# Block 2 of a three-block transformer kernel: gate panels first in the weight stream, head panels rounded at a head's opening, norm statistics in columns

## The reference, cut to what matters

```
u = layer_norm(h) * (1 + sc1) + sh1;   z = u @ w_in          # zq zf zi zg zu zv zga zgb
y_a = hgrn2_mixer(zq, zf, zi, zg) @ w_proj_a                 # 8 heads, a recurrence over 8 chunks
y_b = (gelu(zu) * (W_s LN(gelu(zv)) + b)) @ w_proj_b         # gMLP mixer
mix = (sigmoid(zga + b_a) * y_a + sigmoid(zgb + b_b) * y_b) @ w_out
h   = layer_norm(ALPHA * h + g1 * mix) * ln1_w + ln1_b
```

## Time and profile before

| | us |
|---|---|
| runs | 3443.26, 3445.19, 3452.99 (median 3445.19) |
| profiled execution, its own time | 3450.49 |
| span of its instructions | 3448.7 |
| PE busy | 3134.7 (91%) |
| DVE, ACT, POOL busy | 1843.9 (53%), 1605.0 (47%), 735.3 (21%) |
| granted PE clock, mean | 0.946 of full |
| block 2 up to `out2` | about 813 to 1505 of the span |

### The profile page before, as it was taken

The page is one execution under the profiler, slowest core; times in us unless marked ns, Lnnn a source line. Parts: engine busy times, 40 slices in busy tenths (PEclk is TensorE's granted clock), DMA queues, the critical chain, the costliest instruction groups (busy, mean ns, idle before and its releaser), DMA issues. The chain is left out here.

```text
span 3448.7 us, 38856 instructions
## 1 busy us (share of the span) xinstructions
PE 3134.7 (91%) x13848; PEld 2405.1 (70%) x13848; DVE 1843.9 (53%) x2196; ACT 1605.0 (47%) x2147; POOL 735.3 (21%) x381
## 2 busy tenths in 40 slices
PE   7987899998989888779999884999999999999997
PEld 6754678786777666658888664777777777777753
DVE  3256433426354303361031545888878878888864
ACT  4334444423565322232232422766667666666652
POOL 3400234442323242324444330000000000000020
PEclk9987999999999889899999995999999999999998
DMA  3243322222211021212222614999999999999971
GB/s 142 98 171 117 117 84 97 98 88 84 74 72 50 25 110 49 98 49 97 95 93 106 271 49 197 356 405 400 404 407 402 404 404 398 409 400 403 406 275 49
DMA packets 65734, 694.19 MB, mean 201 GB/s; under 512 B 6928, under 2 KB 7312, under 8 KB 25584
## 3 DMA queue, kind: packets, MB, share of 16 engines
q1 hardware_dynamic: 54480, 650.57, 48.0%
q0 software_dynamic: 7056, 25.69, 1.9%
q10 hardware_dynamic: 4112, 16.78, 1.2%
HBM read 654.74 MB, written 38.27 MB: 201 GB/s over the span
## 5 line engine op out<-in xcount | busy, mean ns | idle before, releaser
L141 POOL TENSOR_TENSOR ring_low<-ring,mix_ring_high 128x1024 fp32r<-128x1024 f32 x120 | 295.3, 2493 | 518.2 <-ACT mix_ring_high L136 518.2
L202 PE MATMUL psum<-mix_high,mix_ring_high 128*128 128x512 f32 x864 | 350.1, 405 | 31.9 <-PEq L1815 11.2
L204 PE MATMUL psum<-mix_high,ring_low 128*128 128x512 f32 x864 | 341.6, 395 | 0.0
L202 PE MATMUL psum<-ex_high,ex_rows_high 128*128 128x512 f32 x768 | 318.3, 414 | 6.8 <-DVE ring_low L2647 6.8
L204 PE MATMUL psum<-ex_high,ex_rows_low 128*128 128x512 f32 x768 | 305.8, 398 | 0.0
L203 PE MATMUL psum<-h_low,mix_ring_high 128*128 128x512 f32 x736 | 291.6, 396 | 0.0
L136 ACT ACTIVATE mix_ring_high<-ring 128x1024 fp32r<-128x1024 f32 x124 | 121.0, 1048 | 334.0 <-DMA ring<-wstream 334.0
L141 POOL TENSOR_TENSOR ring_low<-ring,ff_ring_high 128x1024 fp32r<-128x1024 f32 x72 | 174.8, 2463 | 419.6 <-ACT ff_ring_high L136 227.5
L2478 POOL CAST ex_index<-table 128x1 uint32 x32 | 6.0, 187 | 1083.1 <-PE psum L2496 1083.1
L2647 DVE TENSOR_TENSOR ring_low<-ring,ex_high 128x2048 fp32r<-128x2048 f32 x96 | 214.3, 2287 | 40.3 <-ACT ex_high L2589 40.3
L2647 DVE TENSOR_TENSOR ex_more_low<-ex_more,ex_high_in_x 128x2048 fp32r<-128x2048 f32 x96 | 219.6, 2287 | 22.0 <-ACT ex_high_in_x L2589 22.0
(11 more groups left out here) (551 smaller groups left out, 6897.5 us busy)
## 6 DMA issues: line engine op xcount, KB each, us to landing
ex_more<-moe_w SPq DMA_DIRECT2D x128, 2048.0 KB, 9.4
ring<-wstream SPq DMA_DIRECT2D x87, 2048.0 KB, 8.0
ring<-moe_w SPq DMA_DIRECT2D x64, 2048.0 KB, 10.6
ex_bias_up<-moe_b SPq DMA_DIRECT2D x32, 1024.0 KB, 11.1
y_rows<-ex_y SPq DMA_DIRECT2D x33, 512.0 KB, 10.9
y_rows<-mx_zero ACTq DMA_DIRECT2D x1, 16384.0 KB, 50.0
x<-xt SPq DMA_DIRECT2D x8, 256.0 KB, 4.8
rel<-rel_bias SPq DMA_DIRECT2D x1, 2048.0 KB, 10.4
```

The costliest lines, as they stand in the source:

```text
L141: e.tensor_tensor(low, full, high.bitcast(F32), ALU.subtract).then_inc(self.low_ready, 1)
L202: pe.matmul(out, a[0], b[0], start=start, stop=False)
L204: return pe.matmul(out, a[1], b[0], start=False, stop=stop)
```

## The change

The gate panels come first in each pair of the stream (gate, projection, gate, projection). The first gate panel of mixa is multiplied in body 7 of `hgrn_stage`, as its `following` products; that of mixb in `gmlp_stage` behind L1854, bank by bank as `biased` allows. The gates go to banks 0 to 3 and the projections to 4 to 7; `mix_stage` keeps the panels 1, 2, 3. One more panel load is issued in each of the two stages in front. ACT rounds ring panel n+2 of the head loop at the opening of body n, between taking tile 0 and tile 1 of head n+1, and no longer ahead of the squares. In `gmlp_stage` the gated result `zu` is split tile by tile (ACT highs, DVE lows). The ACT order in `mix_stage` has the four sigmoids ahead of the rounding of panels 2 and 3. `Norm` is new: PE turns the sums into columns (four matmuls of one column for each row of sums, the tokens on partitions), the statistics are made on 128x4, and each is spread again by DVE making four 128x128 diagonals and PE four matmuls of 128 columns with ones. Only n6 keeps the old form (`WideNorm`). In `zi`, the raw norm is spread behind the first four products, and PE's tile 5 waits for `raw_scaled`.

```diff
@@ class Norm (new; the old one is kept as WideNorm)
+    def add_stats(self, pe, tile, at):
+
+        for t in range(TT):
+            mm = pe.matmul(self.stat[:, at + t:at + t + 1], tile[:, t * P:(t + 1) * P], self.g.ones_mean[:, 0:1],
+                           start=True, stop=True)
+        return mm
+
+    def spread(self, pe):
+        if self.centre:
+            for t in range(TT):
+                pe.wait_ge(self.mean_diag, t + 1)
+                mm = pe.matmul(self.mean[:, t * P:(t + 1) * P], self.g.ones, self.diag(0, t), start=True, stop=True)
+            mm.then_inc(self.averaged, 1)
+        for t in range(TT):
+            pe.wait_ge(self.rstd_diag, t + 1)
+            mm = pe.matmul(self.rstd[:, t * P:(t + 1) * P], self.g.ones, self.diag(1, t), start=True, stop=True)
+        mm.then_inc(self.rstd_ready, 1)
+
+    def averages(self, pe):
+        for row in self.rows:
+            mm = self.add_stats(pe, self.g.sums[:, row, :], row * TT)
+        mm.then_inc(self.stat_ready, 1)
+        self.spread(pe)
+
+    def raw_spread(self, pe):
+        for t in range(TT):
+            pe.wait_ge(self.raw_diag, t + 1)
+            mm = pe.matmul(self.raw[:, t * P:(t + 1) * P], self.g.ones, self.diag(0, t), start=True, stop=True)
+        mm.then_inc(self.raw_ready, 1)
+
+    def root(self, act):
+        g = self.g
+        act.wait_ge(self.var_ready, 1)
+        act.activation(self.std, self.var if self.centre else self.square_col, ACT.Sqrt,
+                       bias=g.eps[self.eps if self.before is None else "both"]).then_inc(self.std_ready, 1)
+        if self.before is not None:
+            act.activation(self.raw_std_col, self.raw_col, ACT.Sqrt, bias=g.eps[EPS_RMS]).then_inc(self.raw_std, 1)
+
...
+    def spread_diag(self, dve, i, column, sem):
+        for t in range(TT):
+            dve.tensor_scalar(self.diag(i, t), self.g.ident, column[:, t:t + 1], None, ALU.mult).then_inc(sem, 1)
+
+    def deviations(self, dve):
+        g = self.g
+        dve.wait_ge(self.stat_ready, 1)
+        if not self.centre:
+            dve.tensor_copy(self.square_col, self.stat[:, TT:2 * TT]).then_inc(self.var_ready, 1)
+            return
+        n = len(self.rows) * TT
+        dve.tensor_copy(self.stats[:, 0:n], self.stat[:, 0:n]).then_inc(self.copied, 1)
+        dve.wait_ge(self.copied, 1)
+        dve.scalar_tensor_tensor(self.less, self.mean_col, -1.0, self.mean_col, ALU.mult, ALU.mult).then_inc(self.less_ready, 1)
+        dve.wait_ge(self.less_ready, 1)
+        if self.before is None:
+            dve.tensor_tensor(self.var, self.square_col, self.less, ALU.add).then_inc(self.var_ready, 1)
+        else:
+            dve.tensor_tensor(self.less, self.square_col, self.less, ALU.add).then_inc(self.less_ready, 1)
+            dve.wait_ge(self.less_ready, 2)
+            dve.scalar_tensor_tensor(self.var, self.raw_col, g.eps[self.eps], self.less, ALU.mult, ALU.add).then_inc(self.var_ready, 1)
+        self.spread_diag(dve, 0, self.mean_col, self.mean_diag)
+
+    def apply(self, dve, between=None):
+        body = self.dst if self.centre else self.x
+        dve.wait_ge(self.std_ready, 1)
+        dve.reciprocal(self.inverse, self.std).then_inc(self.inverted, 1)
+        dve.wait_ge(self.inverted, 1)
+        self.spread_diag(dve, 1, self.inverse, self.rstd_diag)
+        if self.centre:
+            dve.wait_ge(self.averaged, 1)
+            for t in range(2):
+                self.centre_tile(dve, t)
+        dve.wait_ge(self.rstd_ready, 1)
...
                     if norm.before is not None:
-                        pe.wait_ge(norm.raw_std, 1)
+                        norm.raw_spread(pe)
                 for i, t in enumerate(tiles):
                     if i < first:
                         continue
+                    if i == 5 and norm is not None and norm.before is not None:
+                        pe.wait_ge(norm.raw_scaled, DT)
...
             def _(pe):
-                def gemm(n, q, m):
+                def gemm(n, q, m, n_is_head=True):
 
                     p = n0 + q
                     pe.wait_ge(gemm_took, n * 4 + m + 1)
@@ -1548,11 +1710,11 @@
                             pe.wait_ge(ring.low_ready, (n - q) * PARTS + PARTS * SPLIT_INDEX[p] + k // (KT // PARTS) + 1)
                         mm = split_product(pe, psum[:, m, :], ring.halves(p, k, m * P, P), tile_halves(high, g.h_low, k),
                                            k == 0, k == KT - 1)
-                    mm.then_inc(gemm_ready, 1)
+                    mm.then_inc(gemm_ready if n_is_head else mix_gate, 1)
 
 
                 def body(n, q, more):
-                    following = lambda m: gemm(n + 1, (q + 1) % 2, m) if more else None
+                    following = lambda m: gemm(n + 1, (q + 1) % 2, m, more)
                     following(0)
                     following(1)
                     pe.wait_ge(head_done, n + 2)
@@ -1570,7 +1732,8 @@
                         mm = pe.transpose(psum[:, 5, t * P:(t + 1) * P],
                                           keys[:, NSUB, 2 * t:2 * t + 2, :].rearrange("p n c -> p (n c)"), g.ident)
                     mm.then_inc(turned, 1)
-                    following(2)
+                    if more:
+                        following(2)
                     pe.wait_ge(key_t_ready, n + 1)
                     pe.wait_ge(vh_ready, n + 1)
                     for c in range(NCH - 1):
@@ -1579,7 +1742,7 @@
                         mm = pe.matmul(psum[:, 6 + c % 2, c // 2 * P:(c // 2 + 1) * P], key_t[half, c // 2, :],
                                        vh[half, q, c // 2, :], start=True, stop=True)
                     mm.then_inc(u_ready, 1)
-                    following(3)
+                    following(3 if more else 2)
                     pe.wait_ge(masked, n * 2 + 2)
                     pe.wait_ge(q_ready, n * 2 + 2)
                     for t in range(TT):
@@ -1591,17 +1754,20 @@
                     mm.then_inc(o_ready, 1)
                     pe.wait_ge(squared, n + 1)
                     pe.matmul(psum[:, 4, :], g.ones, sq, start=True, stop=True).then_inc(sq_summed, 1)
+                    if not more:
+                        following(3)
 
                 for m in range(4):
                     gemm(0, 0, m)
                 every_head(pe, body)
                 for n in range(HH):
                     ring.freed[n0 + n] = (gemm_ready, 4 * (n + 1))
+                ring.freed[n0 + HH] = (mix_gate, 4)
 
             @block.sync
             def _(sp):
                 g.clear_past(sp)
-                ring.load_until(sp, n0 + HH + SLOTS)
+                ring.load_until(sp, n0 + HH + SLOTS + 1)
 
+                def split_panel(n, q):
+                    p = n0 + SLOTS + q
+                    act.wait_ge(gemm_ready, n * 4 + 4)
+                    act.wait_ge(ring.landed[p % SLOTS], (n - q) * 8 + 16 * (p // SLOTS + 1))
+                    for full, high_part, _ in ring.split_parts(p):
+                        act.activation(high_part, full, ACT.Copy).then_inc(ring.high_ready, 1)
+
                 def body(n, q, more):
                     if more:
                         take(n + 1, (q + 1) % 2, 0)
+                    split_panel(n, q)
+                    if more:
                         take(n + 1, (q + 1) % 2, 1)
                     act.wait_ge(turned, n + 1)
                     act.activation(key_t[:, :, :].rearrange("p t k -> p (t k)"), psum[:, 5, :], ACT.Copy).then_inc(key_t_ready, 1)
@@ -1664,11 +1839,6 @@
                         take(n + 1, (q + 1) % 2, 2)
                         decays(n + 1)
                         take(n + 1, (q + 1) % 2, 3)
-                    p = n0 + SLOTS + q
-                    act.wait_ge(gemm_ready, n * 4 + 4)
-                    act.wait_ge(ring.landed[p % SLOTS], (n - q) * 8 + 16 * (p // SLOTS + 1))
-                    for full, high_part, _ in ring.split_parts(p):
-                        act.activation(high_part, full, ACT.Copy).then_inc(ring.high_ready, 1)
...
-                ring.load_until(sp, FIRST["w_mix_b"] + SLOTS)
+                ring.load_until(sp, n0 + SLOTS + 1)
+                ring.high_until(act, n0 + SLOTS)
+                act.wait_ge(mixed, HH)
+                act.wait_ge(rest_ready, HH)
+                for n in range(HH):
+                    act.wait_ge(gated, n + 1)
+                    act.activation(tile_of(zu_high, n), tile_of(zu, n), ACT.Copy).then_inc(zu_rounded, 1)
+                for m in range(4):
+                    pe.wait_ge(biased, m + 1)
+                    for k in range(KT):
+                        if m == 0:
+                            ring.wait_part(pe, n0, k)
+                        mm = split_product(pe, psum[:, m, :], ring.halves(n0, k, m * P, P), tile_halves(*halves, k),
+                                           k == 0, k == KT - 1)
+                    mm.then_inc(mix_gate, 1)
+                def low_of(n):
+                    dve.wait_ge(zu_rounded, n + 1)
```

(51 more changed lines are left out.)

112 lines of the change are left out of this document (95 added, 17 removed).

## The result

| | before | after |
|---|---|---|
| runs, median (us) | 3447.89 (3443.26 to 3452.99) | 3345.22 (3344.12 to 3349.53) |
| span of the profiled execution | 3448.7 | 3343.8 |
| PE busy | 3134.7 (91%) | 3128.2 (94%) |
| granted PE clock, mean | 0.946 | 0.960 |

The account below looks back on a forecast made before the run. The prediction took PE, busy 91% of the span, to be bound by its work plus holes and the low clock behind them. Gains of 24.5, 32, 31.5 and 4 (norms) sum to 92 us: 3353 us, range 3335 to 3377.

Parts of the forecast that it names:

- the last head and the mix stages: Last head with mixa, and gmlp_stage, mixb, out2: PE's holes mostly go and its clock recovers, 32 and 31.5 us less.
- the heads: Head loop: moving the panel rounding off the squares' path cuts the period from 34.8 to 31.3 us, 24.5 over seven holes.

Follow-up runs that it names:

- e8: The changed kernel with the squares of each head made three times instead of once: median 3362.90 us, ratio 0.9743 to the kernel before.
- e9: The changed kernel with POOL's four subtracts in bodies 0 to 6 waiting until DVE has made the key: median 3377.83 us, ratio 0.9787 to the kernel before.
- e7: The changed kernel with the squares of each head made twice instead of once: median 3350.67 us, ratio 0.9711 to the kernel before.

## What to carry to other kernels

A wait names who came last, not why it was late: where the last one is a merge or a rounding, follow the chain to the transfer behind it and see when its queue issued it, since a ring frees its slots in the order of use and one late reader holds back every load behind it. Work that an in-order engine does just ahead of what PE waits for can be moved to where its input has long been there; then look at which of DVE's operations its follower (here POOL's subtracts) meets, because the same four subtracts cost 0.5 us of hole at one place in the head and 3.1 at another. Independent products put behind the last matmul of a stage cover the tail of the other engines, as long as the tail is shorter than they are.

## What the runs showed of the hardware that I had not expected

- Idle time of PE alone does not tell whether the clock falls: at the same hole of 2.4 us it was granted 1.00 once and 0.57 another time in e8, stayed at 1.00 behind 2.66 us ahead of mixa in the changed kernel and was 0.65 behind the same hole in e9 (1173.50 to 1177.50), stayed up behind head 0's 2.7 us in e7 and fell behind its 2.1 in the changed kernel, and fell behind one of four holes of 1.8 us in e7. Behind the heads' holes of 1.2 us it never fell in these runs. So it is to be priced by a chance: one slow head costs 1.1 us net where a hole follows it.
- Of DVE's operations only some are held up by POOL's subtracts of 128x1024 (2.4 us each): tensor_scalar 128x512 from 0.43 to 2.50 us, 128x128 from 0.22 to 2.09, the scans from 1.62 to 2.43 and from 1.19 to 3.33, while the state updates that read PSUM keep their 0.35 us.
- A quarter of the gain is the clock's: 25 of 95 us in the stretch, though the forecast had counted only 11 of 63.5 us for the last head and the mix stages and about 6 of 24.5 in the heads.
